# Modulation pieces in threes behind fewer weight blocks, and wide rounded products in one norm's wait

## The chip, the core and the metric

The kernel runs on one core of a Trainium2 chip. The metric is device time in microseconds (us), the median of several executions. The core's engines run side by side and wait for each other on semaphores: TensorE (PE; its weight loads are PEld), VectorE (DVE), ScalarE (ACT), GpSimd (POOL) and SyncE (SP). Transfers are started from the queues of SP, ACT and POOL and carried out by 16 DMA engines.

## What is computed

Two blocks of a network over 256 tokens of width 1024, one after the other, in float32. The change lies in the first, which has two layers. Cut to what matters:

```python
c_act = jax.nn.silu(c)                       # c: one row of 1024
for layer in range(2):
    mod = c_act @ ada_w[layer] + ada_b[layer]          # 1024 x 6144 weights a layer
    shift_m, scale_m, gate_m, shift_f, scale_f, gate_f = split(mod, 6)
    h = rmsnorm(x, norm_g[layer, 0]) * (1 + scale_m) + shift_m
    mix = conv_retention(h) if layer == 0 else s5(h)   # w_in ... w_out | s5, glu
    x = x + gate_m * mix
    h = rmsnorm(x, norm_g[layer, 1]) * (1 + scale_f) + shift_f
    x = x + gate_f * (square(relu(h @ w_fc1[layer])) @ w_fc2[layer])
```

The products with `ada_w` depend on `c` alone, so they can be made at any time before their results are used. The second block (a state-space mixer, an attention layer, two embeddings) is not touched.

## The kernel before

**Blocks.** All large weights come as blocks of 1024 x 256 values, 1 MB each, through a ring of four buffers that SP fills; a buffer is filled again when PE has finished the block three places earlier. A plain block is 16 f32 products of 256 columns (line 1459). A split block is 48 rounded products of 256 columns (lines 1452, 1454 and 1456): ACT rounds the weights (line 844), DVE makes what the rounding left (line 2229), and PE adds up high times high, high times low and low times high. The phases in question are `w_in` (12 blocks, 8 to 11 split), `w_out` (4 blocks, 1 and 2 split), `fc1_0` (16 split blocks, the first of them "swept": three passes, lines 1528, 1534 and 1539) and `fc2_0` (16 plain blocks).

**Modulation pieces.** `ada_w` is cut into 48 pieces of 1 MB. The first eight are made at the start. Piece n, from 8 to 47, is 8 f32 products of PE (`partial_rows`, line 1555), each on 32 columns of the array and 256 columns long; four of them stand side by side. The table `ADA_AT` says how many pieces PE does behind each block; `pieces_at` turns it into numbers. POOL loads the pieces into three buffers, in order: the transfer of piece n starts when PE has done piece n-3 (line 796). With piece 24 it also loads `s5_c` (1 MB). SP loads `s5_b` (1 MB) ahead of the third block of `fc1_0` (line 764).

**Groups of eight.** After pieces 15, 23, 31, 39 and 47 ACT copies the summed row (line 931); ahead of the next piece PE turns that row into columns (`turned_rows`, line 1564), and ACT copies those into `mods` (line 927). Number 48 is only the last turning. ACT does these copies at the place in its own order where `ADA_AT` puts the piece.

**Around the first feed-forward layer.** Behind the last `w_out` block stand, on PE in this order, a piece and two pieces of phase `norm_1`, the products that sum the squares (line 1601), two more pieces, and the swept block of `fc1_0`. ACT squares `x` (line 888) after its row copies and after it has rounded two blocks of `fc1_0`; DVE lowers one of these blocks before it adds the last part of `w_out` to `x`. Between the blocks of `fc1_0` and `fc2_0` PE also turns tables for the S5 layer (`s5_turned`, line 1781, behind blocks 7, 11, 15 and later ones) and makes S5 kernels (lines 1802 and 1809). ACT stores these tables to DRAM (`we_dram`, `ca_dram`, `k_dram`). Behind blocks 7, 11 and 15 the pieces stand between the two halves of `s5_turned`.

**Products in a wait.** While a norm waits for its reciprocal root, PE makes constant products whose result nobody reads (`idle_products`, line 1588): five f32 ones of 256 columns after the sums of norm 2, 3 and 7. Norms are counted from 0; norm 3 stands ahead of `fc1_1`, the feed-forward layer of the second layer.

Of the kernel before, what the change touches and what calls it, by code (L numbers as in the profile page):

```python
# [25 lines left out]
P = 128  # L26
# [54 lines left out]
COPIES = 32  # L81
ADA_GROUPS = ADA_PIECES // PIECES

ADA_AT = {"w_in": (0, 0, 0, 1, 1, 1, 1, 1, 1, 1, 1), "retention": (1, 1, 1, 1, 1), "w_out": (1, 1, 1, 1), "norm_1": (2, 2),
          "fc1_0": (1,) * 16, "fc2_0": (1,) * 4}


def pieces_at(phase, n=0):

    first = PIECES  # L90
    for name, counts in ADA_AT.items():
        if name == phase:
            first += sum(counts[:n])
            return range(first, first + counts[n])
        first += sum(counts)
    raise KeyError(phase)
# [136 lines left out]
def program(nc, dram, out):  # L233
# [8 lines left out]
    with ctx:  # L242
# [5 lines left out]
        def sb_both(name, shape):  # L248

            offset = -(-nc.sbuf_base // 32) * 32  # L250
            tensor = sb(name, shape)
            twins[tensor.name] = nc.alloc_sbuf_tensor_at(f"{name}_rounded", shape, F32R, offset=offset)
            return tensor
# [17 lines left out]
        mixT = sb_both("mixT", [P, 2 * MT, T])  # L271
# [15 lines left out]
        STAT, MISC = PS[4], PS[5:8]  # L287
# [37 lines left out]
        def squares(i):  # L325

            return hid[:, 0:DT] if i in (3, 7) else sq

        def rounded(x):

            return bass.AP(tensor=twins[x.tensor.name], offset=x.offset, ap=x.ap)
# [160 lines left out]
        def carve(buf, at, *shape):  # L492
            n = int(np.prod(shape))
            v = buf[:, at:at + n]
            if len(shape) == 2:
                v = v.rearrange("p (a b) -> p a b", a=shape[0])
            elif len(shape) == 3:
                v = v.rearrange("p (a b c) -> p a b c", a=shape[0], b=shape[1])
            return v, at + n
# [21 lines left out]
        def mix_tile(k):  # L521

            return conv[:, k] if k < MT else ret[:, k - MT]


        (s5_lr, _, s5_dt, s5_a, s5_th, s5_mag, s5_k, s5_r, s5_sin, s5_cos, s5_abr, s5_abi, s5_nr, s5_den, s5_rden,
         s5_fr, s5_fi, s5_t1, s5_t2) = (s5_small[:, n] for n in range(19))
        s5_lr_raw, s5_li, s5_logdt = (s5_small[:, n] for n in range(20, 23))
        powers, _ = carve(we_t[:, :, :, :].rearrange("p a b c -> p (a b c)"), 0, 2, L + 1, GROUPS)
# [53 lines left out]
        final_sum, _ = carve(ada_sum_flat, 0, 2, T)  # L583
# [7 lines left out]
        ple_early, _ = carve(ada_sum_flat, 1024, DT // 2, T)  # L591
# [6 lines left out]
        ssm_small, _ = carve(we_flat, at, SSM_SMALL)  # L598
# [23 lines left out]
        group_squares, _ = carve(ada_w_flat, 0, 2 * 4, T)  # L622
# [15 lines left out]
        hid_high, _ = carve(more, 0, FT, T)  # L638
        y_high, _ = carve(more, 4096, Z_TILES, T)
        att_high, _ = carve(more, at_probs_end, ATT_TILES, T)  # L640
# [73 lines left out]
        def _(sp):  # L714
# [25 lines left out]
            def load_near(n):  # L740
# [4 lines left out]
                for j in range(L):  # L745
                    sp.dma_start(s5_near[n][GC * j:GC * j + GC],
                                 k_dram[n].rearrange("(q c) x a -> c q (x a)", q=4)
                                 [0:GC, :, 4 * (L - 1 - j) * GC:4 * (L - 1 - j) * GC + 4 * P]).then_inc(near_here[n % 2], 16)

            for b, (name, _, nb) in enumerate(plan):  # L750
                if b < TOGETHER:
                    continue
# [664 lines left out]
        def _(pe):  # L1417
# [167 lines left out]
            def idle_products(i, count):  # L1585

                for _ in range(count):
                    nc.tensor.matmul(MISC[2 if i == 4 else 0][:, 0:T], ident, const[:, 0:T], start=True, stop=True)

            def norm_stats(i):  # L1590

                if i > 0:
                    pe.wait_ge(rstd_ready, i)
                idle_products(i, {7: 4}.get(i, 0))
                tiles = [k for k in range(DT) if k < 2 or k // 2 >= summed.get(i, 1)]
                for k in tiles:
                    if k == 0 and i in summed:
                        pe.wait_ge(sq_sum, sums_until[i])
                    elif k % 2 == 0:
                        pe.wait_ge(sq_ready, sq_before[i] + k // 2 + 1)  # L1600
                    last = nc.tensor.matmul(STAT[:, 0:T], ones, squares(i)[:, k], start=(k == 0), stop=(k == DT - 1))  # L1601
                last.then_inc(stat_ready, 1)
                if i in (2, 3, 7):
                    idle_products(i, 5)
                if i == 8:
                    idle_products(i, 1)

# [47 lines left out]
            pe.wait_ge(c_ready, 1)  # L1655
            first_columns(0)
            norm_stats(0)
            first_turned(0)
            first_columns(1)
# [108 lines left out]
            for piece in pieces_at("norm_1", 0):  # L1768
                modulation(piece)
            norm_stats(1)  # L1770
            for piece in pieces_at("norm_1", 1):
                modulation(piece)
# [55 lines left out]
            def after_block(j):  # L1828

                if j < len(ADA_AT["fc2_0"]):  # L1830
                    for n in pieces_at("fc2_0", j):
# [10 lines left out]


            norm_stats(2)

            for kh in range(2):
                for j in range(L):
                    for b in range(4):
                        k, lo = 4 * kh + b, NCH * b
                        if j == 0:  # L1850
# [3 lines left out]
                                                ident, start=True, stop=True)  # L1854
# [68 lines left out]
            for n in range(4):  # L1923
# [8 lines left out]
                for a in range(4):  # L1932
# [3 lines left out]
                    for part in range(3):  # L1936
                        for q in range(4):
# [3 lines left out]
                            else:  # L1941
                                lhs, rhs = states[:, n % 2, part - 1, g], far[:, part - 1, g % 8]
                            last = nc.tensor.matmul(ps[32 * q:32 * q + 32, P * a:P * a + P], lhs, rhs,
                                                    start=(part == 0), stop=(part == 2))
# [61 lines left out]
            for m in range(XBC_UNITS):  # L2006
# [4 lines left out]
                if m == 0:  # L2011
                    pe.wait_ge(small_here, 16)
                    pe.wait_ge(dt_w_low, 1)
                    for i in range(TT):
                        for k in range(KB):
                            for n, (x, w) in enumerate(((sq, dt_w_high), (hT, dt_w_high), (sq, dt_w))):
                                last = nc.tensor.matmul(MISC[0][:, SSM_HEADS * i:SSM_HEADS * i + SSM_HEADS],
                                                        rounded(x[:, k, P * i:P * i + P]), rounded(w[:, k]),
                                                        start=(k == 0 and n == 0), stop=(k == KB - 1 and n == 2))
                    last.then_inc(dt_psum, 1)  # L2020
                if m == 2:
# [3 lines left out]
                    for i, w in enumerate((less, tri)):  # L2025
                        nc.tensor.matmul(MISC[1][:, SSM_HEADS * i:SSM_HEADS * i + SSM_HEADS], w, dta[:, i], start=True,
                                         stop=True)
                    for i, w in enumerate((less, tri)):
                        last = nc.tensor.matmul(MISC[2][0:SSM_HEADS, P * i:P * i + P], dta[:, i], w, start=True,
                                                stop=True)  # L2030
# [1130 lines left out]
```

## Time and profile before

| | |
|---|---|
| time, median of 3 executions | 1177.98 us (1172.93 to 1179.79) |
| span of the profiled execution | 1171.0 us (its own time around the span is not given; the shortest time above is 1.9 us longer) |
| PE busy | 1112.6 us (95%) |
| DVE, ACT, POOL busy | 816.0 us (70%), 557.7 us (48%), 44.6 us (4%) |
| mean granted TensorE clock | 0.985 of 2.4 GHz |
| moved by DMA | 246.46 MB, 210 GB/s over the span |

In the views a row of the timeline is start, duration, engine, line and names (out<-in); "x16" is how many records were merged. A plain f32 product shows as two records. What stands in brackets is how long the engine was idle before the row, and what ended that. The chain is the work that ended last, followed back from the end.

### The profile page before, as it was taken

What the parts mean: (1) busy time and instruction counts of PE and PEld (TensorE: products, weight loads), DVE (VectorE), ACT (ScalarE), POOL (GpSimd) and SP (SyncE); (2) the same over time, 40 slices, a digit from 0 to 9 for tenths busy, and PEclk for the clock granted to TensorE, in tenths of its full rate; (3) what the DMA queues carried; (4) which work ended last, traced back from release to release, by engine and by line L of the source; (5) the groups of instructions that cost most, each with busy time, mean ns of one, the idle gap of its engine ahead of it and who ended that gap; (6) DMA issues with size and microseconds to landing.
All of it is one profiled execution on the core that took longest, in us unless ns stands there. A gap on an engine that the chain in (4) does not pass through costs nothing.

```text
span 1171.0 us, 22089 instructions
## 1 busy us (share of the span) xinstructions
PE 1112.6 (95%) x9466; PEld 995.9 (85%) x9466; DVE 816.0 (70%) x1390; ACT 557.7 (48%) x876; POOL 44.6 (4%) x71
## 2 busy tenths in 40 slices
PE   6899898999999997879999999999999999999998
PEld 4778686988888885469999999999988899988898
DVE  1599466877578674875666654478899966659955
ACT  3224633445111124554555543356568846467944
POOL 0010001000000000000000000000000000042000
PEclk8999999999999998999999999989989999999999
DMA  9887688899848957865355555525433345343342
GB/s 369 356 280 269 250 323 315 305 339 328 335 182 258 342 186 165 323 245 184 140 184 182 183 189 185 187 81 180 145 109 114 130 153 177 131 153 117 108 145 72
DMA packets 38290, 246.46 MB, mean 210 GB/s; under 512 B 4400, under 2 KB 5584, under 8 KB 9648
## 3 DMA queue, kind: packets, MB, share of 16 engines
q1 hardware_dynamic: 29072, 182.36, 45.7%
q0 software_dynamic: 6240, 43.94, 10.0%
q10 hardware_dynamic: 2880, 18.74, 3.9%
q8 instruction: 75, 1.23, 0.4%
q14 instruction: 23, 0.19, 0.1%
HBM read 225.24 MB, written 19.79 MB: 209 GB/s over the span
## 4 chain that ended last, share of the span: by engine, by line
PE 78%; DVE 10%; DMA 5%; ACT 5%; issue 2%; SPq 0%; ACTq 0%; DVEq 0%
PE ps L1452 16%; PE ps L1454 15%; PE ps L1456 15%; PE ps L1459 10%; PE ps L1555 4%; DMA ca_dram<-more 2%; PE ps L1648 1%; PE ps L1528 1%; PE ps L2083 1%; PE ps L1601 1%; PE ps L1539 1%; PE ps L1534 1%; DMA more<-in_ada_w 1%; DVE ring_rounded L2229 1%; DMA ada_more<-in_ada_w 1%
## 5 line engine op out<-in xcount | busy, mean ns | idle before, releaser
L1452 PE MATMUL ps<-sq_rounded,w_high_rounded 128*128 128x256 f32 x1184 | 341.6, 288 | 2.5 <-DVE mixT_rounded L2236 1.3
L1456 PE MATMUL ps<-sq_rounded,ring_rounded 128*128 128x256 f32 x1184 | 336.2, 284 | 0.0
L2229 DVE TENSOR_TENSOR ring_rounded<-ring,w_high_rounded 128x1024 fp32r<-128x1024 f32 x220 | 260.6, 1226 | 92.1 <-ACT w_high_rounded L844 91.8
L1454 PE MATMUL ps<-hT_rounded,w_high_rounded 128*128 128x256 f32 x992 | 282.1, 284 | 0.0
L844 ACT ACTIVATE w_high_rounded<-ring 128x1024 fp32r<-128x1024 f32 x220 | 219.8, 1049 | 67.0 <-PE ps L1456 66.3
L1452 PEld LDWEIGHTS ps<-sq_rounded,w_high_rounded 128*128 128x128 f32 x1184 | 228.5, 193 | 11.0 <-issue 6.7
L1456 PEld LDWEIGHTS ps<-sq_rounded,ring_rounded 128*128 128x128 f32 x1184 | 228.6, 193 | 0.0
L1454 PEld LDWEIGHTS ps<-hT_rounded,w_high_rounded 128*128 128x128 f32 x992 | 191.8, 193 | 0.1
L1452 PE MATMUL ps<-more_rounded,w_high_rounded 128*128 128x256 f32 x448 | 127.4, 284 | 0.4 <-issue 0.3
L1456 PE MATMUL ps<-more_rounded,ring_rounded 128*128 128x256 f32 x448 | 126.8, 283 | 0.0
L1459 PE MATMUL ps<-big,ring 128*128 128x256 f32 x544 | 121.0, 381 | 0.0
L1459 PEld LDWEIGHTS ps<-big,ring 128*128 128x128 f32 x544 | 102.1, 190 | 14.7 <-issue 1.2
L1454 PE MATMUL ps<-big_rounded,w_high_rounded 128*128 128x256 f32 x384 | 108.7, 283 | 0.0
L1452 PEld LDWEIGHTS ps<-more_rounded,w_high_rounded 128*128 128x128 f32 x448 | 86.0, 192 | 1.1 <-issue 0.7
L1456 PEld LDWEIGHTS ps<-more_rounded,ring_rounded 128*128 128x128 f32 x448 | 86.0, 192 | 0.0
L1454 PEld LDWEIGHTS ps<-big_rounded,w_high_rounded 128*128 128x128 f32 x384 | 73.7, 192 | 0.1
L1454 PE MATMUL ps<-mixT_rounded,w_high_rounded 128*128 128x256 f32 x256 | 72.4, 283 | 0.0
L1022 ACT ACTIVATE big<-ps 128x512 f32<-128x512 f32 x32 | 19.1, 597 | 104.9 <-PE ps L1456 97.2
L1454 PEld LDWEIGHTS ps<-mixT_rounded,w_high_rounded 128*128 128x128 f32 x256 | 49.1, 192 | 0.1
L2342 DVE SCALAR_TENSOR_TENSOR big<-big,cols 128x256 f32<-128x256 f32 x120 | 48.0, 476 | 0.0
L1041 ACT ACTIVATE we_t<-ps 128x512 f32<-128x512 f32 x32 | 17.4, 596 | 58.0 <-PE ps L1781 58.0
L1459 PE MATMUL ps<-hT,ring 128*128 128x256 f32 x192 | 42.7, 381 | 0.0
(426 smaller groups left out, 1640.3 us busy)
## 6 DMA issues: line engine op xcount, KB each, us to landing
ring<-in_blocks SPq DMA_DIRECT2D x139, 1024.0 KB, 4.9
ada_w<-in_ada_w POOLq DMA_DIRECT2D x27, 1024.0 KB, 7.7
ada_more<-in_ada_w POOLq DMA_DIRECT2D x13, 1024.0 KB, 7.6
we_dram<-we_t ACTq DMA_DIRECT2D x8, 1024.0 KB, 8.3
ca_dram<-more ACTq DMA_DIRECT2D x8, 1024.0 KB, 11.9
ring<-we_dram SPq DMA_DIRECT2D x8, 1024.0 KB, 5.5
ring<-ca_dram SPq DMA_DIRECT2D x8, 1024.0 KB, 6.8
big<-in_ada_w SPq DMA_DIRECT2D x4, 1024.0 KB, 10.9
```

What stands on the lines that cost most here:

```text
L844: nc.scalar.activation(w_high[:, c % 2, ks], ring[:, b % RING, ks], ACT.Copy)\
L1022: nc.scalar.activation(hid[:, 2 * n:2 * n + 2], unit(phase, n), ACT.Relu).then_inc(hid_relu, 1)
L1041: nc.scalar.activation(we_t[:, 2 * b:2 * b + 2].rearrange("p g r x -> p (g r x)"), MISC[b % 2][:, :], ACT.Copy).then_inc(we_copied, 1)
L1452: nc.tensor.matmul(out, high[:, k, columns], x_high, start=start, stop=False, skip_group_check=True)
L1454: nc.tensor.matmul(out, high[:, k, columns], x_low, start=False, stop=False, skip_group_check=True)
L1456: last = nc.tensor.matmul(out, low[:, k, columns], x_high, start=False, stop=stop, skip_group_check=True)
L1459: last = nc.tensor.matmul(out, w[:, k, columns], x, start=start, stop=stop, skip_group_check=True)
L1528: nc.tensor.matmul(ps[:, i], high[:, k, P * i:P * i + P], x_high[:, k], start=(k == 0 and i == 0), stop=False, skip_group_check=True)
L1534: nc.tensor.matmul(ps[:, i], low[:, k, P * i:P * i + P], x_high[:, k], start=False, stop=False, skip_group_check=True)
L1555: last = nc.tensor.matmul(bank[j:j + COPIES, 0:NB], c_spread[:, k, PIECES - 1 - piece:PIECES - 1 - piece + COPIES], w[:, k], start=(piece ...
L2229: nc.vector.tensor_tensor(rounded(w), w, w_high[:, c % 2, ks], ALU.subtract)\
L2342: ins = nc.vector.scalar_tensor_tensor(out=conv[:, k], in0=apad[:, k, tap:tap + T], scalar=w, in1=conv[:, k], op0=ALU.mult, op1=ALU.add)
```

## The change

`ADA_AT` gets other numbers: the pieces of `w_in`, `w_out`, `fc1_0` and `fc2_0` mostly come in threes, behind fewer blocks. The five of `retention` and the four of `norm_1` stay, and so does the total. Behind norm 3's sums eight rounded products of 512 columns take the place of the five f32 ones of 256.

```diff
-ADA_AT = {"w_in": (0, 0, 0, 1, 1, 1, 1, 1, 1, 1, 1), "retention": (1, 1, 1, 1, 1), "w_out": (1, 1, 1, 1), "norm_1": (2, 2),
-          "fc1_0": (1,) * 16, "fc2_0": (1,) * 4}
+ADA_AT = {"w_in": (0, 0, 0, 0, 0, 3, 0, 0, 3, 0, 2), "retention": (1, 1, 1, 1, 1), "w_out": (0, 3, 0, 1), "norm_1": (2, 2),
+          "fc1_0": (0, 0, 3, 0, 1, 0, 0, 3, 0, 0, 0, 3, 1, 1, 0, 3), "fc2_0": (3, 0, 1, 1)}
...
+            def wide_idle_products(count):
+
+                for _ in range(count):
+                    nc.tensor.matmul(MISC[0][:, :], rounded(mixT[:, 0, 0:P]), rounded(mixT[:, 1:3]), start=True, stop=True)
+
...
-                if i in (2, 3, 7):
+                if i in (2, 7):
                     idle_products(i, 5)
+                if i == 3:
+                    wide_idle_products(8)
```

The change adds seven lines, so lines from 1593 on have numbers up to 7 higher after it. In the rows below line 1555 is a piece; `ada_w` and `ada_more` are the buffers that it reads.

PE between the split blocks 1 and 2 of `w_out`, before:

```order
L1456 MATMUL ps<-sq_rounded,ring_rounded 128x256
L1555 MATMUL ps<-ada_more 32x256 x8
L1452 MATMUL ps<-sq_rounded,w_high_rounded 128x256
L1454 MATMUL ps<-mixT_rounded,w_high_rounded 128x256
L1456 MATMUL ps<-sq_rounded,ring_rounded 128x256
```

The same place after:

```order
L1456 MATMUL ps<-sq_rounded,ring_rounded 128x256
L1555 MATMUL ps<-ada_w,ada_more 32x256 x8
L1555 MATMUL ps<-ada_more 32x256 x8
L1555 MATMUL ps<-ada_w,ada_more 32x256 x8
L1452 MATMUL ps<-sq_rounded,w_high_rounded 128x256
```

Pieces 21, 22 and 23 now stand together here; before, 21 stood behind block 0, 22 here and 23 behind block 2.

PE from the end of `fc1_0` into `fc2_0`, before (line 1781 is `s5_turned`, 1459 a plain block, 1802 and 1809 an S5 kernel):

```order
L1781 MATMUL ps<-const,more 128x128 x8
L1555 MATMUL ps<-ada_w,ada_more 32x256 x8
L1781 MATMUL ps<-const,more 128x128 x8
L1459 MATMUL ps<-big,ring 128x256 x16
L1555 MATMUL ps<-ada_w,ada_more 32x256 x8
L1459 MATMUL ps<-big,ring 128x256 x16
L1555 MATMUL ps<-ada_more 32x256 x8
L1802 MATMUL ps<-more 32x112 x32
```

After (here 1788 is `s5_turned`, 1809 and 1816 the kernel):

```order
L1788 MATMUL ps<-const,more 128x128 x8
L1555 MATMUL ps<-ada_w,ada_more 32x256 x16
L1555 MATMUL ps<-ada_more 32x256 x8
L1788 MATMUL ps<-const,more 128x128 x8
L1459 MATMUL ps<-big,ring 128x256 x16
L1555 MATMUL ps<-ada_w,ada_more 32x256 x16
L1555 MATMUL ps<-ada_more 32x256 x8
L1459 MATMUL ps<-big,ring 128x256 x16
L1809 MATMUL ps<-more 32x112 x32
```

Pieces 41 to 43 and pieces 44 to 46 now stand one plain block apart; before, 44 stood behind block 15 of `fc1_0` and 45 and 46 behind the first two blocks of `fc2_0`.

## Rows read from the trace of the kernel before

**Rows 1.** The page, chain that ended last: its shares by engine.

```profile
PE 78%; DVE 10%; DMA 5%; ACT 5%; issue 2%; SPq 0%; ACTq 0%; DVEq 0%
```

**Rows 2.** The chain in order of time (start us, us, what), `w_in` and `w_out`.

```profile
45.64 13.81 PE ps L1459 x64
...
60.45 7.11 PE ps L1459 x32
...
150.39 1.00 PE ps L1555 x16
...
157.34 1.00 PE ps L1555 x16
```

**Rows 3.** The timeline of PE, two pieces in a row at the start.

```profile
20.66 1.07 PE L1555 MATMUL ps<-big,ada_more 128*32 128x256 f32 x16
21.55 1.05 PE L1555 MATMUL ps<-more,ada_more 128*32 128x256 f32 x16
```

**Rows 4.** Stretches: busy us and records by engine, granted clock, DMA share, GB/s.

```profile
24.00:44.00 20.00, 16.80 (x129) 12.83 (x128) 6.36 (x24) 6.50 (x15) 1.71 (x3) 1.00 1.02 418
154.00:164.00 10.00, 10.00 (x91) 9.28 (x91) 6.48 (x34) 0.00 (x0) 0.53 (x1) 1.00 0.94 373
164.00:174.00 10.00, 9.73 (x71) 7.51 (x69) 5.64 (x23) 7.30 (x10) 0.53 (x1) 1.00 0.98 369
180.00:183.40 3.40, 3.02 (x8) 1.83 (x6) 0.00 (x0) 0.34 (x1) 0.53 (x1) 0.50 1.04 417
620.00:640.00 20.00, 20.00 (x169) 20.00 (x168) 13.50 (x16) 11.42 (x15) 0.00 (x0) 1.00 0.59 196
```

**Rows 5.** The timeline of PE from the last `w_out` block to the swept block.

```profile
174.03 1.07 PE L1555 MATMUL ps<-ada_more 128*32 128x256 f32 x16 [0.30 <-ACT mods L927]
178.61 1.07 PE L1555 MATMUL ps<-ada_w,ada_more 128*32 128x256 f32 x16 [3.51 <-DMA ada_w<-in_ada_w]
179.61 3.41 PE L1601 MATMUL ps<-sq,const 128*128 128x256 f32 x8
183.68 1.07 PE L1555 MATMUL ps<-ada_w,ada_more 128*32 128x256 f32 x16 [0.65 <-DMA ada_w<-in_ada_w]
185.95 1.07 PE L1555 MATMUL ps<-ada_more 128*32 128x256 f32 x16 [1.20 <-DMA ada_more<-in_ada_w]
186.95 2.18 PE L1528 MATMUL ps<-sq_rounded,w_high_rounded 128*128 128x256 f32 x16
```

**Rows 6.** The timeline of ACT, then of DVE, in the same stretch.

```profile
165.35 0.38 ACT L931 ACTIVATE ada_more<-ps 128x256 f32<-128x256 f32 x1 [15.62 <-PE ps L1555]
...
177.03 0.63 ACT L888 ACTIVATE sq<-xT 128x512 f32<-128x512 f32 x1 [3.05 <-DVE xT L2275]
...
184.53 3.31 ACT L853 ACTIVATE sq_rounded<-hT,mods 128x256 fp32r<-128x256 f32 x8 [0.55 <-DVE hT L2585]
...
173.86 2.35 DVE L2229 TENSOR_TENSOR ring_rounded<-ring,w_high_rounded 128x1024 fp32r<-128x1024 f32 x2
```

**Rows 7.** DMA issues (KB each, us to landing): 76 to 78 us, then 305 to 309 us.

```profile
ada_more<-in_ada_w POOLq DMA_DIRECT2D x1, 1024.0 KB, 7.0
...
ada_w<-in_ada_w POOLq DMA_DIRECT2D x1, 1024.0 KB, 10.5
...
ca_dram<-more ACTq DMA_DIRECT2D x1, 1024.0 KB, 14.2
```

**Rows 8.** The timeline of PE, end of `fc1_0` and first block of `fc2_0`.

```profile
304.80 1.07 PE L1555 MATMUL ps<-ada_w,ada_more 128*32 128x256 f32 x16
...
306.73 7.07 PE L1459 MATMUL ps<-big,ring 128*128 128x256 f32 x32
```

**Rows 9.** The timeline of PE, then of ACT, at norm 3.

```profile
569.64 2.32 PE L1588 MATMUL ps<-const 128*128 128x256 f32 x10
571.97 3.21 PE L1528 MATMUL ps<-sq_rounded,w_high_rounded 128*128 128x256 f32 x16
...
571.31 3.31 ACT L853 ACTIVATE sq_rounded<-hT,mods 128x256 fp32r<-128x256 f32 x8 [0.55 <-DVE hT L2721]
```

## The prediction

> **What bounds the kernel now.** I read the page's chain that ended last first. PE holds 78% of it [rows 1], and PE is busy for 95% of the span, so time on PE counts nearly one for one, except where PE waits. Next I read the chain in order of time through `w_in` and `w_out`, where the pieces stand as links of their own [rows 2]; the reader sees there that a piece isn't hidden under anything. Then the stretches, for what transfers can deliver [rows 4], and the timeline of PE ahead of the first feed-forward layer [rows 5]. There PE waits three times for a piece's transfer (3.51, 0.65 and 1.20 us), and the swept block begins at 186.95, when piece 28 is done. This stage is bound by DMA, not by PE. Last I read the end of `fc1_0` [rows 8], where the new order asks for transfers faster than the old one, and norm 3 [rows 9].
>
> **Fewer piece sites.** Two plain blocks with nothing between them are one link of 13.81 us, 6.91 a block; a block with a piece at either side takes 7.11, and the piece 1.00 [rows 2]. A piece beside plain blocks so costs 1.00 + 0.20 = 1.2 us. Beside split blocks it is the same: from piece 21 to piece 22 are 157.34 - 150.39 = 6.95 us [rows 2], and the 48 products between them take 48 x 0.12 = 5.76, at 20.00 us for 169 records [rows 4], which leaves 1.19. Of two pieces in a row, the second begins 0.89 after the first [rows 3]. Every site that joins another so saves 1.2 - 0.89 = 0.3 us. Sites go from 8 to 3 in `w_in`, 4 to 2 in `w_out`, 16 to 7 in `fc1_0` and 4 to 3 in `fc2_0`: 17 sites and 5.1 us, of which 1.5, 0.6, 2.7 and 0.3 us lie in the four phases. The other end is 0: no row shows three pieces in a row with their waits. I take 0.3, because the pair in [rows 3] is the same work on the same buffers.
>
> **The stage that DMA bounds.** The saving in `w_in` and `w_out` (2.1 us) reaches the swept block only if transfers keep up, since piece 28 releases it [rows 5]. Piece n may be fetched when piece n-3 is done. Before, pieces 24, 25 and 26 could start after 21, 22 and 23, that is at 151.4, 158.3 [rows 2] and about 165.3, where ACT's row copy is released by piece 23 [rows 6]. Now all three follow block 1 of `w_out`. That block ends at 157.34 - 1.5 - 1.2 = 154.6 (the saving of `w_in`, and piece 21 no longer ahead of it), so they start at about 155.5, 156.4 and 157.3: one of them 4 us later, the others 2 and 8 us earlier. The queue is empty ahead of them, and no transfer catches up what isn't asked for. Before, 11 transfers of 1 MB (five pieces, `s5_c`, `s5_b`, four ring blocks) lay between 150.4 and 185.9, 3.23 us each with everything around them. Now ten of them lie behind 154.6, because one ring block is through by then: at 3.23 us the last lands at 186.9, 1.0 us later than before. By the rate of the two stretches in the middle, 373 and 369 GB/s [rows 4], one takes 2.8 us; ten of them end at 182.6 with no start-up, and at 186.8 with all that a landing of 7.0 us [rows 7] has beyond 2.8. At 418 GB/s [rows 4] one takes 2.5 us and the two ends are 179.6 and 184.1, some 182 in the middle. I take the first, **+1.0**, as it holds the pauses of this very stage, and -4 (the 182) to +1 as bounds.
>
> What else could bind there comes earlier and is hidden. ACT's 15.62 us of waiting for piece 23 [rows 6] end some 8 us sooner, so its rounding of the next blocks and its squares come earlier. DVE lowers a block (2.35 us) ahead of the residual on which the last square waits 3.05 us [rows 6]; that lowering is released earlier too, so I put the squares some 4 us earlier and the sums that now begin at 179.61 [rows 5] at about 175. ACT's rounding follows the sums by about 1.5 us (183.0 to 184.53 [rows 5, 6]), so it would be ready near 178. Piece 28 is later than that at any of the rates.
>
> With the sums earlier and piece 28 not, PE's pause ahead of pieces 27 and 28 grows. Between 180.0 and 183.4 the granted clock is 0.50 [rows 4], the lower of the two levels, after PE's waits of 3.51 us and more [rows 5]. A stretch of this length at half clock over the swept passes would cost 3.4 / 2 = 1.7 us; at none of it 0. I take **+0.6**, a third, since before it lay mostly on the sums and cost nothing there.
>
> **fc1_0 and fc2_0.** Sites save 2.7 + 0.3 = **-3.0**. But behind block 15 of `fc1_0` stand 41 to 43, and 44 to 46 only one block on. Call U the time when 41 is done. Then 44 to 46 are asked for at U, U + 0.9 and U + 1.8, and PE reaches 44 after the other two (1.8), half of `s5_turned` (0.9) and a plain block (7.0) [rows 8]: 44 at U + 9.7, 46 at U + 11.5. A piece takes 7.0 us to land in calm and 10.5 at the place in question [rows 7]; each of the next two adds 2.8. So 46 lands at U + 12.7 or at U + 16.2, and PE waits 1.2 or 4.7 us. Before, 44 stood ahead of the block [rows 8] and nothing waited. I take the middle, **+3.0**: the 10.5 stands in the right place, but there the piece left beside ACT's stores. Behind the waiting PE on its queue stands block 1 of `fc2_0` or the S5 kernel; ACT and DVE wait for these, and none of them can give the time back, because PE is the bound. The threes behind blocks 2, 7 and 11 have four or five blocks of 6 us between them and pay nothing (their transfers lie under those blocks; without that cover the same 1 to 5 us).
>
> **Norm 3.** Eight rounded products of 512 columns take 8 x 2 x 0.12 = 1.9 us at the rate above, in place of 2.32 [rows 9]. The swept block behind them is paced by ACT: the rounding that it eats begins at 571.31 and lasts 3.31 us [rows 9], so an earlier start of PE changes nothing: **0**. Bounds: -0.3 if the first pass starts earlier and ends so; +3.8 if a column costs what it does in f32 (8 x 0.93 = 7.4 us, to 577.1, and 16 products after that).
>
> **Sum.** +1.0 + 0.6 - 3.0 + 3.0 + 0 = +1.6 us on the span of 1171.0, so 1172.6. The median of the runs shown is 7.0 above that span; with the same distance the time is 1179.6.
>
> **A rule weighed.** Pieces leave from POOL's queue, ring blocks from SP's and the tables from ACT's. At 305 to 309 us a piece takes 10.5 us in place of 7.0, and ACT's table of 1 MB issued beside it 14.2 [rows 7]; neither came at the full rate first. The Trainium skill ("DMA: Bandwidth & Descriptors", section "Queues, rings and completion order") says that each DMA engine goes round the queues that have work for it, a packet at a time; the rows agree as far as they go. By that rule three pieces in one queue share with the two other queues and don't get the whole rate, which is the third of the rivals below.
>
> **Rivals.**
>
> *Transfers keep up.* Piece 28 lands near 182.0 and 46 in time: -3.9 - 3.0 = -6.9, a time of 1171.1. For it speaks the 418 GB/s of the early stretch, with DMA engines always supplied [rows 4], and that three requests now come at once. Against it: 373 and 369 GB/s in this stage with DMA at 94% and 98% busy [rows 4].
>
> *Pieces 44 to 46 wait by turns with ACT's stores* (the side of slower). If 44 takes the 14.2 us of the store [rows 7] and the next two 2.8 each, 46 lands at U + 19.9 and PE stands 8.4 us in place of 3.0; a low clock afterwards adds up to 1.7. That is +1.6 + 5.4 + 1.7 = +8.7, a time of 1186.7. It decides from the point where a store of 1 MB is in flight when 43 is done. For it: such a store leaves ACT within 3 us of a piece there already [rows 7]. Against: the stores come behind the second half of `s5_turned` and 44 is asked for ahead of it. By the skill's rule above this is the outcome, if the stores begin within the first 3 us.
>
> *The pieces don't run together*, because each of the three waits for a transfer or a copy of its own. Then the 3.0 us of sites are gone: +4.6, a time of 1182.6. Against it: they were fetched a block or more before.
>
> **How the numbers follow.** Forecast 0.55, transfers keep up 0.20, turns 0.20, no joining 0.05. A measurement of this kernel tells about 0.5% (5.9 us) from no change: below 1172.1 is faster, above 1183.9 slower. Keeping up lies at the lower bound (0.13 faster, 0.07 same), turns beyond the upper one (0.17 slower, 0.03 same), no joining near it (0.03 same, 0.02 slower), and of the forecast, whose own range by its terms is 1175 to 1183, I leave 0.03 on either side: faster 0.16, same 0.62, slower 0.22. The range goes from 1170, below the keeping up, to 1187, above the turns.
>
> **What would show it.** In the changed kernel's PE timeline: waits for DMA ahead of pieces 26 to 28, and the swept block at 187 to 188 (at 183 the transfers kept up); waits ahead of 44 to 46 behind the first block of `fc2_0`, 1 to 5 us in sum (none, and the forecast is 3 us too long; 8, and it is the turns); three pieces in 2.9 us with their site; the swept block of norm 3 ending where it did relative to ACT's rounding. It would be wrong if the granted clock falls in other places, or if ACT's or DVE's tables, which move with the pieces, become late for PE in the S5 layer.

## The result, and the profile after

The changed kernel takes 1179.99 us (median of 20 executions, 1174.88 to 1183.16), the kernel before 1175.78 us (20, 1171.81 to 1179.85). The ratio is 1.0035, with a 95% interval of 1.0022 to 1.0047: slower by 4.1 us, within 0.5% as forecast (1179.6, likeliest case "within 0.5%"). That the number was met so closely is luck in part: the forecast was a change of +1.6 us and the change is +4.1, while the median of three executions that it started from (1177.98) lies 2.2 us above the median of twenty (1175.78). One of the twelve executions of the kernel of experiment 7 below took 6087 us; it is left out of its ratio, and nothing on record says what held it.

The profiled executions lie further apart than the medians, 1178.7 against 1171.0 us. PE's busy time grew by 3.5 us only, while the granted clock falls at different places in the two pages. More on that below.

The place that costs the time is behind the first block of `fc2_0`. PE's waits there, in the changed kernel (what PE waited for, us in total, times, longest):

```profile
PE ps L1555 <- DMA ada_more<-in_ada_w: 3.9, 1, 3.9
PE ps L1555 <- DMA ada_w<-in_ada_w: 0.2, 1, 0.2
```

And the timeline of PE there, which answers to [rows 8]:

```profile
312.66 1.07 PE L1555 MATMUL ps<-ada_w,ada_more 128*32 128x256 f32 x16
313.91 1.07 PE L1555 MATMUL ps<-ada_w,ada_more 128*32 128x256 f32 x16 [0.18 <-DMA ada_w<-in_ada_w]
318.93 1.94 PE L1555 MATMUL ps<-ada_more 128*32 128x256 f32 x16 [3.95 <-DMA ada_more<-in_ada_w]
```

Pieces 44 and 45 are there or nearly so; 46 is 3.95 us late, and then takes 1.94 us in place of 1.05, because the clock has fallen. The issues between 302 and 309 us show who shared the transfers (engine, KB each, us to landing):

```profile
ada_w<-in_ada_w POOLq DMA_DIRECT2D x2, 1024.0 KB, 7.8
ada_more<-in_ada_w POOLq DMA_DIRECT2D x1, 1024.0 KB, 13.8
we_dram<-we_t ACTq DMA_DIRECT2D x1, 1024.0 KB, 9.9
ca_dram<-more ACTq DMA_DIRECT2D x1, 1024.0 KB, 19.2
k_dram<-more ACTq DMA_DIRECT2D x1, 480.0 KB, 15.7
```

Piece 46 (`ada_more`) landed 13.8 us after its issue, and ACT's stores moved beside it. It was asked for at 305.12, and the first store left at 306.54:

```profile
305.12 0.53 POOL L796 DMA_DIRECT2D ada_more<-in_ada_w  x1 [0.34 <-PE ps L1555]
...
306.54 0.33 ACTq L1047 DMA_DIRECT2D we_dram<-we_t  x1
```

DMA was busy all the while: in the stretch with the lower clock behind the wait (columns as in [rows 4]) it stands at 1.00 and 419 GB/s.

```profile
318.00:322.00 4.00, 3.07 (x19) 1.62 (x20) 0.00 (x0) 0.00 (x0) 0.00 (x0) 0.58 1.00 419
```

Ahead of the first feed-forward layer, where [rows 5] showed PE waiting for transfers, it waits in the same three places (line 1606 is the products that sum the squares):

```profile
176.01 1.07 PE L1555 MATMUL ps<-ada_more 128*32 128x256 f32 x16 [0.30 <-ACT mods L927]
178.95 1.94 PE L1555 MATMUL ps<-ada_w,ada_more 128*32 128x256 f32 x16 [1.87 <-DMA ada_w<-in_ada_w]
180.81 2.62 PE L1606 MATMUL ps<-sq,const 128*128 128x256 f32 x8
185.69 1.93 PE L1555 MATMUL ps<-ada_w,ada_more 128*32 128x256 f32 x16 [2.27 <-DMA ada_w<-in_ada_w]
187.99 1.51 PE L1555 MATMUL ps<-ada_more 128*32 128x256 f32 x16 [0.36 <-DMA ada_more<-in_ada_w]
189.43 2.18 PE L1528 MATMUL ps<-sq_rounded,w_high_rounded 128*128 128x256 f32 x16
```

In `w_in` there are two waits that the kernel before does not have (50 to 110 us, the whole answer):

```profile
PE ps L1699 <- ACT more L964: 0.9, 1, 0.9
PE ps L1487 <- DVE ring_rounded L2236: 0.6, 1, 0.6
```

At norm 3 the eight wide products begin at 576.18 and the swept block at 578.70, after a wait of 0.32 for ACT's rounding, as [rows 9] led to expect: PE is there first, and ACT sets the pace.

```profile
576.18 2.19 PE L1593 MATMUL ps<-mixT_rounded 128*128 128x512 f32 x8
578.70 3.21 PE L1528 MATMUL ps<-sq_rounded,w_high_rounded 128*128 128x256 f32 x16 [0.32 <-ACT sq_rounded L853]
```

To read off where the time comes from, I laid the instructions of PE in the two traces side by side and took the difference of their starts at chosen places. From 59 us on, ahead of the first piece of `w_in`, to 345 us, and without what the clock did at 127 us, it moves so: `w_in` +0.3 us, `w_out` -0.7, the stage from the last `w_out` block to the swept block +0.5, `fc1_0` -2.7, the pieces 44 to 46 +6.2 (beyond what the moved piece itself takes), everything else there about 0. That is +3.3 us with -0.3 for the site of `fc2_0`, near the +4.1 of the medians. Behind 345 us the two profiles move another 2 us apart, mostly where the clock falls in that of the changed kernel (at 520 and 779 us).

### The profile page after: what moved, and what is told of

Same layout as the page of the kernel before. It is cut to its first block, busy times and chain, and to the rows that moved or that the text cites. A ratio compares the mean times of both kernels' runs of the same rounds, so it can differ in the third digit from the quotient of the medians.

```text
span 1178.7 us, 22085 instructions
## 1 busy us (share of the span) xinstructions
PE 1116.1 (95%) x9464; PEld 1002.5 (85%) x9464; DVE 816.1 (69%) x1390; ACT 557.7 (47%) x876; POOL 44.6 (4%) x71
## 4 chain that ended last, share of the span: by engine, by line
PE 72%; DVE 14%; DMA 6%; ACT 5%; issue 3%; SPq 0%; ACTq 0%; DVEq 0%
PE ps L1452 15%; PE ps L1456 15%; PE ps L1454 15%; PE ps L1459 7%; PE ps L1555 3%; DMA ca_dram<-more 2%; DVE big L2349 2%; DMA ada_more<-in_ada_w 2%; DVE ring_rounded L2236 1%; PE ps L1655 1%; PE ps L1528 1%; DVE ada_more L2859 1%; PE ps L2090 1%; PE ps L1606 1%; PE ps L1539 1%
## 6 DMA issues: line engine op xcount, KB each, us to landing
ada_more<-in_ada_w POOLq DMA_DIRECT2D x13, 1024.0 KB, 10.5
ca_dram<-more ACTq DMA_DIRECT2D x8, 1024.0 KB, 12.9
```

## The experiments

All ratios are to the kernel before. Experiments 1 and 2 undo or isolate parts of the change; what they expect speaks of two theories, the late transfers of pieces 44 to 46 against a granted clock that the threes pull down. The expectations call some kernels by name: e1_tail_later is that of experiment 1, e8_fc_tail_later (or e8) of 5, e12_no_28_ahead of 7 and e11_w_in_elsewhere of 8. Each kernel has one profile, which is one execution.

**1. Pieces 44 to 46 one block later** (the changed kernel otherwise).

```diff
-"fc2_0": (3, 0, 1, 1)}
+"fc2_0": (0, 3, 1, 1)}
```

> The changed kernel with one number moved: pieces 44 to 46 stand behind the second block of fc2_0 and not behind the first. Theory (transfers of 44 to 46 are late by 4 to 5 us, and that is what makes the change slower): there is one block of 7 us more, so the waits ahead of 45 and 46 (0.2 and 4.0 us) and the half clock behind them are gone; 4 to 6 us faster than the changed kernel, that is within 1.5 us of the kernel before. Rival (the loss comes from the granted clock falling in w_in and retention, and the wait only takes the place of others): under 2 us faster than the changed kernel, over 2 us slower than before.

Measured: 1172.52 us, ratio 0.9977 (0.9959 to 0.9996). That is 6.8 us under the changed kernel, by the ratios 1.0035 - 0.9977 = 0.0058, and faster than the kernel before. No wait for a piece stands between 190 and 345 us any more. The theory of the late transfers holds. Its price is 6.2 us in the trace, where PE's starts move from 2.05 to 8.26 us ahead of the changed kernel across the place; the intervals of the two ratios leave the 4 to 6 us open.

**2. One part of the change alone.** Three kernels: only `w_in` and `w_out`, only `fc1_0` and `fc2_0`, only the wide products.

```diff
+ "w_in": (0, 0, 0, 0, 0, 3, 0, 0, 3, 0, 2), "w_out": (0, 3, 0, 1)
```

> The kernel before with the new numbers of w_in and w_out alone. Theory (the stage ahead of the swept block is bound by transfers): the sites' 2.1 us are lost there, and the swept block begins within 1.5 us of 186.95; time within 1.5 us of before. Rival (threes pull the granted clock down ahead of 130 us, as the profile of the changed kernel shows it at 43 and at 128 us): half clock shows at these places again, and the time is 2 to 4 us longer than before.

Measured: 1175.03 us, ratio 0.9998 (0.998 to 1.0016). No change. A fall of the clock at 44 to 48 us (0.57) does stand in its profile, and none at 128 (1.00); that profile is of the longest of its twelve executions, 1180.09 us, and yet the median is that of before, so the fall is no price of the change. The swept block begins at 191.88 there and not within 1.5 us of 186.95: 2.6 us of the 4.9 stand already at 59 us, ahead of the first piece of `w_in`, and 1.2 are a wait for a piece in `retention`.

```diff
+ "fc1_0": (0, 0, 3, 0, 1, 0, 0, 3, 0, 0, 0, 3, 1, 1, 0, 3), "fc2_0": (3, 0, 1, 1)
```

> The kernel before with the new numbers of fc1_0 and fc2_0 alone. Theory: 10 fewer sites give 3.0 us back up to the first block of fc2_0, the waits ahead of 45 and 46 there take 4 to 6 us; 1 to 3 us slower than before. Rival (the clock in w_in is the loss): 0 to 1 us slower.

Measured: 1180.05 us, ratio 1.0038 (1.002 to 1.0056). The whole loss of the change is in this part. It is 4.5 us and not 1 to 3: a wait of 4.29 us ahead of piece 46, and a stretch of low clock behind it (0.57 from 317 to 325 us) that my sum had left out. Its trace also settles the clock at 42 and 126 us. Up to 190 us this kernel is the kernel before, and in its profile (first two rows) the granted clock falls in two stretches where that of the kernel before (last two rows, first column of numbers after POOL) stays at 1.00:

```profile
42.00:46.00 4.00, 4.00 (x14) 3.31 (x13) 0.37 (x2) 0.95 (x2) 0.00 (x0) 0.67 1.01 416
...
126.00:130.00 4.00, 3.71 (x10) 3.01 (x11) 0.20 (x1) 0.34 (x2) 0.00 (x0) 0.57 0.56 227
```

```profile
42.00:46.00 4.00, 4.00 (x19) 3.54 (x20) 1.48 (x9) 2.69 (x5) 0.00 (x0) 1.00 1.02 424
126.00:130.00 4.00, 3.63 (x24) 3.42 (x25) 0.93 (x3) 1.87 (x4) 0.00 (x0) 1.00 0.56 231
```

So these two falls, which the changed kernel's profile has as well, differ between executions of the same instructions, and are not its doing.

```diff
-                if i in (2, 3, 7):
+                if i in (2, 7):
                     idle_products(i, 5)
+                if i == 3:
+                    wide_idle_products(8)
```

> The kernel before with eight rounded products of 512 columns in place of the five f32 ones in norm 3's wait, and nothing else. Theory: the swept block is paced by ACT's rounding, so no difference, within 1 us of before. Rival (products of the other kind change the granted clock behind them): 1.5 us or more either way, with the half-clock stretch that stands at 520 us or the one at 774 us at another place.

Measured: 1174.03 us, ratio 1.0001 (0.9983 to 1.0019). No difference, as expected. Its clock falls where that of before does not (33 to 37 us, long ahead of norm 3, at 0.57), which again is not the edit's doing; the stretch at 774 us, behind norm 3, is where it was.

**3. Which of the three pieces is late.** The changed kernel with 44 and 45 behind block 0 and 46 behind block 1.

```diff
-"fc2_0": (3, 0, 1, 1)}
+"fc2_0": (2, 1, 1, 1)}
```

> The changed kernel with 44 and 45 behind the first block of fc2_0 and 46 behind the second. In the changed kernel 44 landed ahead of its place, 45 0.2 us late and 46 4 us late. Theory (it is the third transfer alone that is late): wait under 1 us, no half clock behind the block, 5 to 7 us faster than the changed kernel. Rival (any group that follows three pieces after one block pays, since the stores of ACT take their turns): still 2 us or more of waiting ahead of 45, and 2 to 4 us faster only.

Measured: 1174.17 us, ratio 0.9992 (0.9975 to 1.0009), 5 us under the changed kernel. The waits view shows no wait for a piece there; the two pieces take 2.20 us where they take 1.93 with nothing between:

```profile
314.80 2.20 PE L1555 MATMUL ps<-ada_w,ada_more 128*32 128x256 f32 x32
```

It is the third transfer alone that costs.

**4. Why it is late.** The changed kernel, with ACT's three stores held back until the first block of `fc2_0` is done.

```diff
                     copy_weights(turn, (2, 3))
-                    store_weights(turn)
+                    if n < 15:
+                        store_weights(turn)
...
+            act.wait_ge(blocks_done, first_block["fc2_0"] + 1)
+            store_weights(2)
             store_kernels(1)
             store_outputs(2)
```

> The changed kernel with ACT's three stores at the end of fc1_0 (one table to we_dram, k_dram, ca_dram, 1 MB each) held back until the first block of fc2_0 is done, some 6 us later; pieces 44 to 46 stay behind that block. Theory (pieces wait by turns with ACT's stores): 46 lands within 11 us of its issue and not 13.8, the wait of 4 us ahead of it is under 1 us, the time 3 to 6 us below the changed kernel, less what the later tables cost DVE. Rival (POOL's queue gives 4.5 to 5 us for each of three pieces by itself): 46 lands 13 us or more after its issue, the wait stays at 3 us or more.

(`k_dram` is 480 KB, as the rows above show, and not the 1 MB written there.) Measured: the issues between 302 and 309 us are

```profile
ada_w<-in_ada_w POOLq DMA_DIRECT2D x2, 1024.0 KB, 6.5
ada_more<-in_ada_w POOLq DMA_DIRECT2D x1, 1024.0 KB, 8.9
```

8.9 us in place of 13.8, and the timeline of PE behind the block has no wait (its lines are three higher):

```profile
312.42 1.93 PE L1558 MATMUL ps<-ada_w,ada_more 128*32 128x256 f32 x32
314.17 1.05 PE L1558 MATMUL ps<-ada_more 128*32 128x256 f32 x16
315.15 7.17 PE L1462 MATMUL ps<-big,ring 128*128 128x256 f32 x32
```

Three pieces of POOL's queue by themselves landed 2.5 us apart (308.85, 311.35 and 313.81, from the times of issue and the times to landing; the ring block ahead of them was through at 306.43); with ACT's stores beside them, 4.5 and 5.0 us apart (309.33, 313.87 and 318.89). Time 1174.1 us, ratio 1.0008 (0.9988 to 1.0028), 3 us under the changed kernel by the ratios, the lower end of what was expected, and the two intervals still overlap a little. The trace is clearer: across the place PE's starts move from 0.24 to 6.25 us ahead of the changed kernel, so with the stores gone 6.0 of the 6.2 us are gone. The stores are the cause of the lateness. The rule named in the prediction (the Trainium skill, "DMA: Bandwidth & Descriptors", section "Queues, rings and completion order") would give this; the runs agree as far as landing times can show turns.

**5. The new numbers of fc1_0 and fc2_0 without the stall.** The kernel before, with

```diff
+ "fc1_0": (0, 0, 3, 0, 1, 0, 0, 3, 0, 0, 0, 3, 1, 1, 0, 3), "fc2_0": (0, 3, 1, 1)
```

> The kernel before with the new numbers of fc1_0 and fc2_0 alone, but with 44 to 46 behind the second block of fc2_0. Theory (a joined site gives 0.3 us back): 10 sites, 3.0 us faster than before, as e1_tail_later (the pieces of w_in and w_out then bring nothing). Rival (the gain of e1_tail_later is that of the w_in and w_out sites, and the sites of fc1_0 are given back in waits): 1 us or less.

Measured: 1171.65 us, ratio 0.9965 (0.9947 to 0.9984), 4.1 us faster. Between the swept block and the end of the pieces PE's starts moved from 2.0 us ahead of the kernel before to 5.0 ahead: 3.0 us, what ten joined sites were to give. The third piece still landed 13.1 us after its request here (300.64 to 313.74), beside ACT's stores, but one block more stands ahead of its use. The timeline has the three pieces at their bare price, 2.8 us from first to last:

```profile
315.08 1.93 PE L1555 MATMUL ps<-ada_w,ada_more 128*32 128x256 f32 x32
316.83 1.05 PE L1555 MATMUL ps<-ada_more 128*32 128x256 f32 x16
```

**6. One megabyte less ahead of the swept block.** `s5_c` leaves with piece 19, once in the kernel of experiment 1 and once in the kernel before.

```diff
-                if n == PIECES + 16:
+                if n == PIECES + 11:
                     pool.dma_start(s5_c[:, :, :, :], dram["s5_c"]).then_inc(c_here, 16)
```

> The kernel with 44 to 46 one block later (e1_tail_later), and s5_c (1 MB) loaded with piece 19 and not with piece 24, so that it is through before the stage ahead of the swept block. Theory (that stage is bound by the megabytes that must land before piece 28): nine transfers in place of ten, at 2.9 us each as the changed kernel showed them; piece 28 lands 2 to 3 us earlier relative to the last block of w_out, the waits ahead of pieces 26 to 28 shrink from 4 to 5 us to about 2, and the kernel is 2 to 3 us faster than e1_tail_later (ratio to before about 0.995 to 0.996). Rival (the norm's own chain, squares, sums and rounding, holds the swept block just behind piece 28): under 1 us.

> The kernel before with s5_c loaded with piece 19 and not with piece 24, nothing else. Theory (transfers bind): 2 to 3 us faster than before. Rival (the last square comes at 177.7 and the sums at 178 at the earliest, so the norm's chain takes the place of the transfers): 1 us or less.

Measured: 1172.98 us, ratio 0.999 (0.9972 to 1.0007), against 0.9977 of experiment 1, and 1174.36 us, ratio 0.9991 (0.9973 to 1.0009). Neither shows the 2 to 3 us. In the traces the swept block comes only 1.3 and 1.5 us earlier relative to the end of `w_out` than in the one trace that each is compared with; against the mean of all profiles with the same instructions up to there it is 0.9 us in both (the spread of these follows below). My theory, that the sum of megabytes sets this stage, does not carry. In the first of the two piece 26 was there in time, and PE still waited 4.94 us ahead of piece 27:

```profile
187.33 1.93 PE L1555 MATMUL ps<-ada_w,ada_more 128*32 128x256 f32 x16 [4.94 <-DMA ada_w<-in_ada_w]
```

That transfer is asked for only when PE has done piece 24, behind the last block of `w_out`, and it lands 8.7 us later, with a megabyte less queued ahead. The rival of both expectations, the norm's own chain, does not hold the swept block either: PE waits for pieces 27 and 28 in both traces.

**7. Without the pieces that hold the swept block.** The kernel of experiment 5, with

```diff
+ "norm_1": (2, 0), "fc1_0": (0, 0, 3, 0, 3, 0, 0, 3, 0, 0, 0, 3, 1, 1, 0, 3)
```

> e8_fc_tail_later with pieces 27 and 28 taken out of norm_1, (2, 0) in place of (2, 2), and two more pieces behind block 4 of fc1_0. Nothing needs these two there. Theory (the swept block waits for piece 28, and that for its request behind piece 25, not for the sum of megabytes): the swept block begins when ACT's rounding is ready, some 2 us earlier relative to the end of w_out; the two pieces cost 1.7 us behind block 4, so the time is that of e8 within 1.5 us. Rival (the whole stage is bound by transfers, so that what isn't waited for here is waited for at the next blocks): waits for DMA ahead of the next blocks of fc1_0 or their rounding, and 1 to 3 us slower than e8.

Measured: 1171.35 us, ratio 0.9959 (0.994 to 0.9977). The swept block now waits for the norm's own chain:

```profile
183.91 3.66 PE L1528 MATMUL ps<-sq_rounded,w_high_rounded 128*128 128x256 f32 x16 [2.16 <-ACT sq_rounded L853]
```

It begins 2.9 us earlier than in the kernel before, relative to the last block of `w_out`, and 1.9 us earlier than in experiment 5. No wait for transfers shows up behind it. The time is that of experiment 5 within the intervals, as two more pieces behind block 4 take it back. The two transfers are still asked for where they were (behind pieces 24 and 25); what is gone is their use ahead of the swept block.

**8. The pieces of w_in at other blocks.** The kernel of experiment 5, with

```diff
+ "w_in": (0, 0, 0, 0, 0, 3, 0, 3, 0, 2, 0)
```

> e8_fc_tail_later with the pieces of w_in as (0, 0, 0, 0, 0, 3, 0, 3, 0, 2, 0): three sites as in the changed kernel, but ahead of the first split block (8) and behind the block before the scores, where the changed kernel shows waits of 0.6 us for DVE's lowering and 0.9 us for ACT's copy. Theory (pieces there were cover for DVE and ACT, and taking them away lost the 1.5 us of five joined sites): both waits are gone, and from 59 to 125 us the stretch is 1.0 to 1.5 us shorter than before; time 1 us below e8. Rival (the waits come from something else in the order): 0.6 and 0.9 us stand there still, no difference from e8.

Measured: 1170.35 us, ratio 0.9968 (0.9952 to 0.9985). The trace says yes: PE has no wait at all between 50 and 110 us, and the stretch from 59 to 116 us is 1.6 us shorter than before, where that of the changed kernel is 0.3 longer. The median against experiment 5 can't tell a microsecond (intervals of 2 us either way).

**9. Together**: the kernel of experiment 7 with the pieces of `w_in` as in 8.

> e12_no_28_ahead with the pieces of w_in as in e11_w_in_elsewhere: everything that the runs so far showed to pay, on the kernel before. Theory (the terms add up: 3.0 us of sites in fc1_0 and fc2_0, 1.4 us in w_in that reach the swept block because piece 28 no longer holds it, 2 us there less 1.8 us for two pieces behind block 4): 4.5 to 5 us faster than before, a ratio of 0.9955 to 0.9965; the swept block begins about 2 us after PE reaches it, when ACT's rounding is ready. Rival (the w_in part is lost ahead of the swept block to another wait, on the transfer of piece 26): 3 us, a ratio near 0.9975, with a wait of over 3 us ahead of piece 26.

Measured: 1168.15 us, ratio 0.9944 (0.9923 to 0.9964), faster than both kernels and the fastest of all; 6.6 us by the ratio, more than the 4.5 to 5 us that the terms add up to, which the interval holds; PE's starts gain 5.4 us on the kernel before between 59 and 345 us. The swept block begins at 180.12 and waits for ACT alone, as expected:

```profile
174.96 1.07 PE L1555 MATMUL ps<-ada_w,ada_more 128*32 128x256 f32 x16 [1.66 <-DMA ada_w<-in_ada_w]
...
180.12 3.65 PE L1528 MATMUL ps<-sq_rounded,w_high_rounded 128*128 128x256 f32 x16 [2.17 <-ACT sq_rounded L853]
```

## Why the prediction came out, point by point

**Sites: right in size where nothing hid behind them.** `fc1_0` gave -2.7 us (forecast -2.7), `w_out` -0.7 (-0.6), and experiment 5 gave the -3.0 of both later phases. In `w_in` the step failed: -1.5 was forecast, +0.3 measured. Of the 1.8 us between them 1.5 are the two new waits, 0.6 for DVE's lowering and 0.9 for ACT's copy; the other 0.3 is open. I had asked what hides an edit, but not what a piece hides: ahead of the first split block and ahead of the scores a piece covered the time that DVE and ACT need. Experiment 8 puts pieces back there, and both waits go.

**The stage that DMA bounds: the +1.0 was met by luck, the mechanism was half right.** I let the swept block come at +1.0 us whatever PE saved ahead, because ten transfers must land after a moment that the order sets. One pair of traces can't size this stage. From the start of piece 25 (the row that waits 0.30 us for ACT's `mods`) to the swept block, four profiles with the instructions of before up to there (before, experiment 5 and two of experiment 2) take 12.0 to 12.9 us, mean 12.4, and five with those of after (after, experiments 1, 3 and 4 and one of 2) 13.3 to 14.3, mean 13.9. Experiment 5 stands at the low end, experiment 1 near the high one:

```profile
172.94 1.07 PE L1555 MATMUL ps<-ada_more 128*32 128x256 f32 x16 [0.30 <-ACT mods L927]
...
184.95 2.18 PE L1528 MATMUL ps<-sq_rounded,w_high_rounded 128*128 128x256 f32 x16
```

```profile
172.15 1.07 PE L1555 MATMUL ps<-ada_more 128*32 128x256 f32 x16 [0.30 <-ACT mods L927]
...
186.43 3.13 PE L1528 MATMUL ps<-sq_rounded,w_high_rounded 128*128 128x256 f32 x16
```

So the stage is 1.5 us longer with the new order and not 0.5, and with +0.3 and -0.7 ahead of it the swept block comes 1.1 us later: the forecast, but put together of a saving that was mostly missing (0.4 in place of 2.1) and a stage that grew by 1.5 where the forecast let it grow by 3.1. The load is part of it: piece 28 lands 8.8 to 10.5 us after its request in the four profiles and 10.5 to 11.6 in the five. But its request follows piece 25, hence PE's own progress, and not a moment set by the order ahead; experiment 6 took a megabyte away and got 0.9 us, less than half of the forecast, and nothing that the medians can tell. Experiment 7 took the use of the two pieces away and the wait went to ACT. That the late request sets the rest is read from the landings; no run asked for these pieces earlier. The sums, which I put at about 175, began at 180.81: they stand behind piece 26 on PE, whose transfer came at 178.9.

**The clock term** (+0.6 over the swept passes) is no price of the change. From the first to the last start of the swept block's 48 products there are 5.7 to 7.6 us, 5.7 with the clock at full; the mean is 6.6 in the four profiles and 6.7 in the five. Whether the low clock falls on these passes differs between executions of the same instructions.

**The stall behind the first block of fc2_0: right place, wrong size.** Forecast +3.0 between 1.2 and 4.7; measured 0.18 + 3.95 = 4.1 us of waiting, and 6.2 us with the low clock on piece 46 and the block behind it. Three things were off. The first of the three pieces landed 5.9 us after its request, before ACT's stores took their part, where I had 7.0 to 10.5; each further one took 4.5 to 5.0 us beside the stores, where I added 2.8; and the clock's share stood in the rival alone. So the truth lies between the forecast and the rival of turns (8.4 and 1.7): the rival's mechanism is the right one, as experiment 4 shows, while its price was made from the landing of a store that was itself behind two others. My argument against it, that the stores come behind the second half of `s5_turned`, was weak: they left at 306.5 us, 1.4 us after the request for 46, early enough to take half of the rate.

**Norm 3: 0, and 0 measured.** The median of experiment 2 can't tell less than 2 us (1.0001, 0.9983 to 1.0019), but PE's starts in the changed kernel lie 6.73 us behind those of before ahead of norm 3 (at 566 us) and 6.72 behind it (at 591). PE waits 0.32 us for ACT as the step said. The eight took 2.19 us, 1.9 by the sum.

**Why the total fitted.** The forecast had +1.0 and +0.6 for the front, and -3.0 and +3.0 behind: +1.6. Measured are +1.1 for `w_in`, `w_out` and the stage (mean of the profiles), 0.1 for the clock there, and -3.0 and +6.2 behind: +4.4, against the +4.1 of the medians. The stall was 3.2 us too cheap, the front 0.4 too dear. What closed the gap was the base: the distance of the median to the profiled span, from three executions, was 7.0 us where twenty give 4.8.

## What to carry to other kernels

Filler work on the bounding engine costs its own time (0.89 us a piece here) and something for each place where it stands (0.3 us here), and joining it in fewer places earns only the second: ask of each place what another engine does in its shade, and leave a piece there. Before putting k units of prefetched work in a row, count from the request, which the release of a buffer sets, to the use of the last; beside another queue's stores a piece took 4.5 to 5.0 us here in place of 2.5. A wait ahead of a block that looks like bandwidth may be a late request: take away bytes, and take away the use, in two runs, and see which one moves it. And before a step of half a microsecond is read from two traces, look at how far traces of the same instructions lie apart.

## What the runs showed of the hardware

Identical instructions get a different granted clock from one execution to the next, also on one core alone: in experiment 2 two kernels that are the kernel before up to 190 us have their clock at 0.57 to 0.67 in stretches (33 to 37, 42 to 46, 126 to 130 us) where that of the kernel before has 1.00, and at 42 to 46 us PE is busy for 4.00 of 4 us in either. One such stretch costs 1.6 to 1.7 us here, so the spans of two profiles can't be compared closer than that; the steps between two places can, where no such fall and no wait for a transfer lies between them. Where PE waits for transfers, executions of the same instructions lay up to 1.0 us apart (the stage ahead of the swept block). And three transfers of 1 MB asked for within 2 us landed 2.5 us apart in one queue alone, 4.5 to 5.0 apart beside a second queue with 2.5 MB.
